# Seven half-size products a weight slot in eight late stages of a two-block transformer kernel, on a ring of three slots

## The reference

```
z = proj[..., g_end:].reshape(B_, L, N_BRANCH, N_KV, HPG, HEAD_DIM)
o = jnp.sum(gates * jax.nn.silu(z) * o_br, axis=2)
return o.reshape(B_, L, ATT_WIDTH) @ w_o
...
y_a = _gated_deltanet(q_a, k_a, v_a, z_a, beta_a, dec_a, conv_w[l], a_log[l], dt_bias[l], gdn_o_norm_w[l])
y_b = _moba_attention(q_b, k_b, v_b, q_norm_w[l], k_norm_w[l], rel_bias)
mix = (jax.nn.sigmoid(gate_a) * jnp.einsum('btc,cd->btd', y_a, w_branch_gdn[l])
       + jax.nn.sigmoid(gate_b) * jnp.einsum('btc,cd->btd', y_b, w_branch_moba[l]))
h = h + jnp.einsum('btd,de->bte', mix, w_out[l])
u = _rmsnorm(h, norm_ffn_w[l])
hid = jax.nn.silu(jnp.einsum('btd,df->btf', u, w_ffn_gate[l])) * jnp.einsum('btd,df->btf', u, w_ffn_up[l])
h = h + jnp.einsum('btf,fd->btd', hid, w_ffn_down[l])
```

## Time and profile before

| | |
|---|---|
| median of three runs | 3459.02 us |
| profiled execution, its own time | 3459.03 us |
| span of its core in the trace | 3457.1 us |
| TensorE busy | 3270.6 us, 95% of the span |
| VectorE, ScalarE, GpSimd busy | 1424.6, 474.7, 127.6 us |
| read from HBM | 593.7 MB, 173 GB/s over the span |
| `zc` stage | 1035 to 1148 us |
| attention with `zs` | 1148 to 1485 us |
| `o` and its norm | 1488 to 1620 us |
| `gdn`, `za`, `qb`, `kb`, `vb` | 1620 to 2046 us |
| scan with `ga` | 2046 to 2227 us |
| head norms and `gb` | 2227 to 2300 us |
| moba with `gb2` | 2300 to 2374 us |
| `bra`, `brb`, mix | 2374 to 2494 us |
| `out2` and its norm | 2494 to 2621 us |
| feed-forward part | 2621 to 3457 us |

### The profile page before, as it was taken

The page is one execution under the profiler, slowest core; times in us unless marked ns, Lnnn a source line. Parts: engine busy times, 40 slices in busy tenths (PEclk is TensorE's granted clock), DMA queues, the critical chain, the costliest instruction groups (busy, mean ns, idle before and its releaser), DMA issues.

```text
span 3457.1 us, 50025 instructions
## 1 busy us (share of the span) xinstructions
PE 3270.6 (95%) x20868; PEld 2894.0 (84%) x20868; DVE 1424.6 (41%) x2155; ACT 474.7 (14%) x799; POOL 127.6 (4%) x89
## 2 busy tenths in 40 slices
PE   6999998979999999988999999999898999999999
PEld 4777787868888877777888887688787999999999
DVE  5456625453220233313266731251104555555443
ACT  2114410000000222211220011311000000000000
POOL 0013310000000000011000000000000000000000
PEclk8999999989999999998999999999999999999999
DMA  9764377656563322232235332233432444444443
GB/s 409 296 262 162 157 281 300 249 220 249 228 275 125 139 101 97 97 122 109 111 144 182 149 138 94 98 130 108 172 146 103 168 167 170 170 170 164 172 163 133
DMA packets 50908, 598.73 MB, mean 173 GB/s; under 512 B 9511, under 2 KB 12086, under 8 KB 13278
## 3 DMA queue, kind: packets, MB, share of 16 engines
q1 hardware_dynamic: 50782, 596.88, 44.7%
HBM read 593.70 MB, written 3.16 MB: 173 GB/s over the span
## 4 chain that ended last, share of the span: by engine, by line
PE 84%; DMA 8%; DVE 5%; ACT 1%; DVEq 1%; issue 1%; SPq 0%; ACTq 0%; POOLq 0%; POOL 0%
PE bank L271 29%; PE bank L2037 23%; PE bank L301 13%; DMA ring<-in_t_mod 6%; PE bank L292 5%; PE bank L313 3%; DVE E L341 3%; PE bank L379 1%; PE bank L2051 1%; PE aux L1226 1%; PE aux L1181 1%; DMA ring<-in_t_out 0%; DMA ring<-in_t_kv 0%; DMA ring<-in_t_q 0%; PE aux L861 0%
## 5 line engine op out<-in xcount | busy, mean ns | idle before, releaser
L271 PE MATMUL bank<-arena,ring 128*128 128x256 f32 x3072 | 681.6, 385 | 43.2 <-DVE arena L1955 10.0
L271 PEld LDWEIGHTS bank<-arena,ring 128*128 128x128 f32 x3072 | 592.3, 193 | 129.7 <-issue 29.9
L271 PE MATMUL bank<-hT,ring 128*128 128x256 f32 x2560 | 561.5, 382 | 8.5 <-DVE hT L625 4.6
L271 PEld LDWEIGHTS bank<-hT,ring 128*128 128x128 f32 x2560 | 489.6, 192 | 77.6 <-issue 5.6
L301 PE MATMUL bank<-hT,ring 128*128 128x256 f32 x2304 | 533.0, 384 | 0.0
L301 PEld LDWEIGHTS bank<-hT,ring 128*128 128x128 f32 x2304 | 430.2, 191 | 75.2 <-issue 20.6
L2037 PE MATMUL bank<-arena,ring 128*128 128x128 f32 x3440 | 396.4, 275 | 0.0
L2037 PEld LDWEIGHTS bank<-arena,ring 128*128 128x128 f32 x3440 | 390.2, 192 | 0.0
L2037 PE MATMUL bank<-hT,ring 128*128 128x128 f32 x1680 | 197.9, 275 | 0.0
L2037 PEld LDWEIGHTS bank<-hT,ring 128*128 128x128 f32 x1680 | 192.7, 192 | 0.1
L341 DVE SCALAR_TENSOR_TENSOR E<-ring,c_act,E 128x512 f32<-128x512 f32 x240 | 182.8, 762 | 18.5 <-issue 0.6
(11 more groups left out here) (385 smaller groups left out, 2873.3 us busy)
## 6 DMA issues: line engine op xcount, KB each, us to landing
ring<-in_t_mod SPq DMA_DIRECT2D x64, 2048.0 KB, 13.9
ring<-in_t_gu SPq DMA_DIRECT2D x44, 2048.0 KB, 8.5
ring<-in_t_out SPq DMA_DIRECT2D x16, 2048.0 KB, 8.6
ring<-in_t_zs SPq DMA_DIRECT2D x16, 2048.0 KB, 8.5
ring<-in_t_down SPq DMA_DIRECT2D x16, 2048.0 KB, 7.3
ring<-in_t_gdn SPq DMA_DIRECT2D x12, 2048.0 KB, 8.4
ring<-in_t_u SPq DMA_DIRECT2D x8, 2048.0 KB, 9.9
ring<-in_t_z SPq DMA_DIRECT2D x8, 2048.0 KB, 8.5
```

The source lines that it names most:

```text
L271: last = nc.tensor.matmul(bank[s][:, T * f:T * f + T], w[:, j, P * f:P * f + P], act[:, j, :], start=j == 0, stop=j == kd - 1)
```

## The change

Eight stages (`zc`, `o`, `ga`, `gb`, `gb2`, `bra`, `brb`, `out2`) take their slots as the feed-forward part does: seven products of half the size (`late_split`), in all 37 full slots and 12 half-size ones (`SPLIT`; slot 0 of `o`, `ga`, `bra`, `out2` and slots 0, 4, 7 of `brb` stay plain). From `zc` to the end the ring has three places (`late_raw`), the fourth holds two of the weight sums for two slots (`late_spare`); the other two are written over the slot itself. A place is reloaded as soon as PE is done with it (`late_done`), no longer after the drain, and a slot now has a pair of banks, so that PE waits for the drain of the slot two before (`wait_out`). Two of the four weight sums are made by GpSimd (`pool_sums`) in all of these stages but `o` and `out2`, where VectorE makes them. The attention's and the scan's loops over groups and heads are written out. The sigmoid or SiLU of a split slot is a ScalarE pass over SBUF after VectorE has put the slot together (`late_act`).

The head norms go by rows: the sums of 12 blocks are put in four groups of 32 partitions of three banks (`pe_norm_sums`, 12 matmuls with 32 columns of weights), one root of 128x1536 and two reciprocals (128x512, 128x1024) follow, and three times four matmuls with one row of weights (`pe_norm_wide`) spread them again. `pe_norm_sums` and `pe_bias` stand after `gb`'s slot 0. The mix goes by slot: each slot of `bra` and `brb` is multiplied by its gate, and in `brb` added, as soon as it is done.

```diff
+LATE = [("zc", 8), ("zs", 16), ("o", 8), ("gdn", 12), ("za", 4), ("qb", 4), ("kb", 4), ("vb", 4),
+        ("ga", 8), ("gb", 4), ("gb2", 4), ("bra", 8), ("brb", 8), ("out2", 8)]
+LRING = 3
+LBASE = {n: sum(c for _, c in LATE[:k]) for k, (n, _) in enumerate(LATE)}
+LCOUNT = dict(LATE)
+LSLOTS = sum(c for _, c in LATE)
+EARLY = sum(n for _, n in ORDER)
+SPLIT = {"zc": range(8), "o": range(1, 8), "ga": range(1, 8), "gb": range(4), "gb2": range(4),
+         "bra": range(1, 8), "brb": (1, 2, 3, 5, 6), "out2": range(1, 8)}
+SPLITS = [(n, k) for n, _ in LATE if n in SPLIT for k in SPLIT[n]]
+SPLIT_INDEX = {x: m for m, x in enumerate(SPLITS)}
+ACTED = ("zc", "ga", "gb", "gb2")
+ACT_BASE = {n: sum(len(SPLIT[m]) for m in ACTED[:k]) for k, n in enumerate(ACTED)}
...
+        def late_ready(pe, n):
+            pe.wait_ge(late_in[n % LRING], 16 * (n // LRING + 1))
+            if n < 2:
+                for s in (2 * n, 2 * n + 1):
+                    wait_early(pe, s)
+            else:
+                wait_out(pe, n - 2)
...
+        def late_load(sp, name, k, count=SLOT):
+            n = LBASE[name] + k
+            if n < LRING:
+                wait_early(sp, (EARLY + n) % RING)
+            else:
+                sp.wait_ge(late_done, n - LRING + 1)
+            sp.dma_start(late_raw[n % LRING][:, 0:count], t["t_" + name][k]).then_inc(late_in[n % LRING], 16)
...
+            t1, t2, t3, t4 = t_all
+            one, two = late_bank(n)
+            if first == 0:
+                late_ready(pe, n)
+            end = 7 * half if count is None else first + count
+            for step in range(first, end):
+                q, j = step // half, step % half
+                if step == 0:
+                    pe.wait_ge(halves_ready, halves[0])
+                if q == 2 and j == 0:
+                    pe.wait_ge(late_sums, m + 1)
+                if q == 4 and j == 0:
+                    pe.wait_ge(halves_ready, halves[1])
+                if q == 5 and j == 0:
+                    pe.wait_ge(late_last, m + 1)
+                out, at, a, b = ((one, 0, w[:, 0, 0], x[0][0]), (one, 1, w[:, 1, 0], x[1][0]), (one, 2, s2, t2),
+                                 (two, 0, s1, t1), (two, 1, w[:, 0, 1], t3), (two, 2, w[:, 1, 0], x[1][1]),
+                                 (two, 3, w[:, 1, 1], t4))[q]
+                last = nc.tensor.matmul(out[:, P * at:P * at + P], a[:, j, :], tile_at(b, j),
+                                        start=j == 0 and q in (0, 3), stop=j == half - 1 and q in (2, 6))
+                if j == half - 1 and q == 1:
+                    last.then_inc(late_second, 1)
+                if j == half - 1 and q == 2:
+                    last.then_inc(late_first, 1)
+                if step == 7 * half - 1:
+                    last.then_inc(late_done, 1)
...
+        def late_keep(act, name, k):
+            n, m = LBASE[name] + k, SPLIT_INDEX[name, k]
+            loop_wait(act, late_first, m + 1)
+            nc.scalar.copy(join_keep[n % 2], late_bank(n)[0][:, 0:P]).then_inc(late_kept, 1)
...
+        def dve_sums(dve, name, k, parts=(0, 1)):
+            v, m = nc.vector, SPLIT_INDEX[name, k]
+            n = LBASE[name] + k
+            w, (s1, s2) = late_weights(name, k), late_two_sums(name, k)
+            if (name, k) in POOLED:
+                if 1 in parts:
+                    dve.wait_ge(late_pooled, POOLED.index((name, k)) + 1)
+            elif 0 in parts:
+                if m == 0:
+                    wait_early(dve, (EARLY + LRING) % RING)
+                dve.wait_ge(late_in[n % LRING], 16 * (n // LRING + 1))
+                if m > 1:
+                    old, at = SPLITS[m - 2]
+                    dve.wait_ge(late_done, LBASE[old] + at + 1)
+                v.tensor_tensor(s1, w[:, 0, 1], w[:, 1, 1], ALU.add)
+                dve.drain()
+                v.tensor_tensor(w[:, 0, 1], w[:, 0, 0], w[:, 0, 1], ALU.subtract)
+            if 1 in parts:
+                v.tensor_tensor(s2, s1, w[:, 0, 0], ALU.subtract)
+                dve.drain().then_inc(late_sums, 1)
...
+        POOLED = [(n, s) for n in ("zc", "ga", "gb", "gb2", "bra", "brb") for s in SPLIT[n]]
+        def pool_sums(pool, names):
+            for name, s in POOLED:
+                if name not in names:
+                    continue
+                n, m = LBASE[name] + s, SPLIT_INDEX[name, s]
+                w, (s1, s2) = late_weights(name, s), late_two_sums(name, s)
+                if m == 0:
+                    wait_early(pool, (EARLY + LRING) % RING)
+                pool.wait_ge(late_in[n % LRING], 16 * (n // LRING + 1))
+                if m > 1:
+                    old, at = SPLITS[m - 2]
+                    pool.wait_ge(late_done, LBASE[old] + at + 1)
+                nc.gpsimd.tensor_tensor(s1, w[:, 0, 1], w[:, 1, 1], ALU.add)
+                pool.drain()
+                nc.gpsimd.tensor_tensor(w[:, 0, 1], w[:, 0, 0], w[:, 0, 1], ALU.subtract)
+                pool.drain().then_inc(late_pooled, 1)
...
+        def dve_last_sum(dve, name, k):
+            m, w = SPLIT_INDEX[name, k], late_weights(name, k)
+            dve.wait_ge(late_second, m + 1)
+            nc.vector.tensor_tensor(w[:, 1, 0], w[:, 1, 0], late_two_sums(name, k)[1], ALU.subtract)
+            dve.drain().then_inc(late_last, 1)
+        def dve_join(dve, name, k, to):
+            v, n, m = nc.vector, LBASE[name] + k, SPLIT_INDEX[name, k]
+            one, two = late_bank(n)
+            dst = to.rearrange("p f n -> p (f n)")
+            dve.wait_ge(late_kept, m + 1)
+            v.tensor_tensor(dst[:, 0:P], one[:, P:2 * P], join_keep[n % 2], ALU.add)
+            v.tensor_tensor(join_two, one[:, 2 * P:3 * P], join_keep[n % 2], ALU.add)
+            dve.drain()
+            dve.wait_ge(late_done, n + 1)
+            v.tensor_tensor(join_pair.rearrange("p (a n) -> p a n", a=2), two[:, 0:2 * P].rearrange("p (a n) -> p a n", a=2),
+                            rep(join_two, 2), ALU.add)
+            dve.drain()
+            v.tensor_tensor(dst[:, P:3 * P], two[:, 2 * P:4 * P], join_pair, ALU.add)
+            v.tensor_tensor(dst[:, 3 * P:4 * P], two[:, 0:P], join_pair[:, P:2 * P], ALU.add)
+            dve.drain().then_inc(late_out[n % 2], 1)
...
         def pe_scan(pe):
...
+                def fill(plain, split):
+                    nonlocal done
+                    if h:
+                        late_split(pe, "ga", h, h_quarters, h_halves, (H_H, H_H3), done, split)
+                    else:
+                        late_plain(pe, "ga", h, hT, done, plain)
+                    done += split if h else plain
+                fill(7, 12)
...
+        def dve_norms(dve):
             v = nc.vector
+            v.tensor_scalar(q_scaled, col("q_norm"), SCALE, None, ALU.mult)
+            dve_last_sum(dve, "gb", 0)
+            dve_sums(dve, "gb", 1)
+            dve.wait_ge(norm_roots, 1)
+            v.reciprocal(norm_rows[:, 0:512], norm_rows[:, 0:512])
+            dve.drain().then_inc(norm_inv, 1)
+            v.reciprocal(norm_rows[:, 512:1536], norm_rows[:, 512:1536])
+            dve.drain().then_inc(norm_inv, 1)
+            for s in range(2):
+                dve_join(dve, "gb", s, two_tiles(gb_all, s))
+                dve_last_sum(dve, "gb", s + 1)
+                dve_sums(dve, "gb", s + 2)
+                dve.wait_ge(norm_wide, s + 1)
...
+        def dve_mix(dve):
...
+                if s in SPLIT[name]:
+                    dve_join(dve, name, s, two_tiles(to, s))
+                    v.tensor_tensor(two_tiles(to, s), two_tiles(to, s), two_tiles(gate, s), ALU.mult)
...
+                if name == "brb":
+                    v.tensor_tensor(two_tiles(x, s), two_tiles(x, s), two_tiles(y, s), ALU.add)
+            dve.drain().then_inc(mix_ready, 1)
...
             for n in range(FRING):
-                wait_old(sp, (FIRST_FFN + n) % RING)
+                sp.wait_ge(late_done, LSLOTS - LRING + n + 1)
                 load(n, gu[n])
```

559 lines of the change are left out of this document (399 added, 160 removed).

## The result

The changed kernel takes 3397.22 us (median of four runs, 3396.16 to 3398.61); the kernel before, with one more run, 3457.24. The ratio is 0.9829, 95% interval 0.9812 to 0.9846: 60.0 us less, where 56.4 were forecast (from 3459.02, the median that the forecast had). The profiled execution has a span of 3395.3 us, against 3457.1.

What follows compares the result with a forecast made beforehand. TensorE, 84% of the chain, was taken to bound the kernel. Terms of -56.3, +1.5, -11.1, +0.3, +0.3, +1.8, +5.6 and +1.5 summed to -56.4 from 3459.02: 3402.6 us, range 3384 to 3432.

Steps and rivals of the forecast that it cites:

- Products, -56.3: In the split stages, 37 full slots save 1.31 us each and 12 half-size ones 0.655: -56.3 us.
- Mix, -11.1: Ahead of `out2`, mixing by slot leaves about 2.0 us of 10.03 idle and 3.05 of slow start: -11.1 us.
- Feed-forward start, +5.6: After `out2`, slot 2's later load and four sums delay VectorE's reciprocal, and TensorE waits: +5.6 us (0 to +9).
- Norms, +0.3: Around `gb`, a 6.3 us wait for `rel_in`, bias, spreads, slow start and queries: 17.8 against 17.5, +0.3 us (-6 to +14).
- Equations, +1.2 of the scan's +0.3: At the scan's start, equations 12.8 us later make TensorE idle 2.7 at `ga`: first transpose +1.2; whole scan +0.3 us.
- Moba, +1.8: In moba, 0.9 us for VectorE held up by GpSimd and 0.9 for the bank wait ahead of `bra`: +1.8 (0 to +8).
- GpSimd beside VectorE, +1.5 in `brb`: In `brb`'s five slots, VectorE loses time to GpSimd on the shared port, 0.3 us a slot: +1.5 (bounds nothing to 6.6).
- I cost it at nothing: GpSimd's two sums a slot, outside `o` and `out2`, fit in the slack and cost nothing; without cover, 140 us.
- Rival 2: Norm matmuls run in turn (+14), or a tenth to a quarter of GpSimd's 140 us shows: 3412 to 3438 us; 20%.
- Rival 3: TensorE waits for GpSimd's sums before the third product in six stages: slower, all 140 us giving 3543; 5%.
- Half sums ahead of `zc`, +0.4: At `zc`'s start, a join or a pass is added behind the last product: +0.4 us.
- Attention, +0.5: At the attention's start, a join or a pass is added behind the last product: +0.5 us.

Runs made afterwards that it cites:

- e7: The kernel before, with only the attention's loop over four groups written out on three engines: 3440.20 us, ratio 0.9955.
- all repairs: The changed kernel with equations, tables and root first and GpSimd held back: 3370.58 us; with the norms' reciprocals in three parts as well: 3364.25 us.

## Why the prediction was right, and where it wasn't

The time, its sign and the range hold: 3397.2 against 3402.6 (3384 to 3432). The terms:

- **Products, -56.3: right.** 12.51 and 6.25 us a slot in each stage, also where GpSimd makes two sums; undone in 14 slots they cost 18.3. Only `zc`'s slot 0 gains less (15.1 us against 15.8), since PE's clock is still low there.
- **Mix, -11.1: right.** -8.4 for the gap and -2.8 for `out2`'s start.
- **Feed-forward start, +5.6: right.** +5.2; undone, -6.5.
- **Norms, +0.3: 3 too low, the mechanism right.** The wait for the tables is 5.7 (6.3). Missing were 1.9 of the wait ahead of moba (GpSimd beside VectorE: held back, 2.1 go), 0.9 of the bias product (1.87, at a low clock) and 0.6 of the spreads (1.07 each); the slow start was 2.2 (a slot of 14.7), put at 3.0. That the reciprocals lie bare once the tables are early was worked out at 5 and measured at 4.8.
- **Equations, +1.2 of the scan's +0.3: too low.** The 12.8 us are 14.4, the idle time 4.9 instead of 2.7, and the slow start behind it (1.8) was not in the sum; nor were the wait of 2.0 and the low clock of 1.6 behind it. Head 0 lost 7.3 us in all; the other seven won 2.4 beyond their products, where I had put 2.5 for PE's waits for ScalarE, which are gone.
- **Moba, +1.8: +2.7.** The wait ahead of `bra` is 0.8 (0.9); 1.6 are its first products at a low clock behind the wait for VectorE, which the sum did not have; what the sum had, 0.9 for VectorE held up, is then at most 0.3.
- **GpSimd beside VectorE, +1.5 in `brb`: the wrong place and size.** In `brb` it is 0.1. The runs tie some 11 us to it elsewhere: waits of 8.6, ahead of `zc`, in head 0 and ahead of moba, and 2.8 at a low clock behind the first two. The step that failed is "I cost it at nothing" and its slack, which asked only whether the sums come in time. They do: PE never waits for them. But where VectorE has a row of sums of its own on PE's path and GpSimd has two slots to catch up on, each VectorE sum waits for one of GpSimd's: 3.2 us instead of 1.2. Rows 6 gave the price (up to one GpSimd instruction each time they meet); I counted the meetings in the stages and not at their starts. Rival 2, which also rested on rows 6, meant another thing, slots that grow because the sums come late, and that didn't happen. Rival 3's break-even is miscounted: 56.4 us over 35 slots are 1.6 us a slot; the 4 that the prediction gives are all 140.
- **Half sums ahead of `zc`, +0.4: wrong**, +3.4, for that reason. At 1.23 us each they are hidden under the gates.
- **Attention, +0.5: wrong**, -7.2. I had passed over "loops written out" for the attention. It moves ScalarE's table load ahead of a wait, and PE's four waits at the groups' ends get 6.4 us shorter. I had taken this for the scan alone, as "half of 5.2", without its cause.
- **End of `o`, +0.6: -0.2**, nothing.
- **`gdn` to `vb`, nothing: -4.2,** of which 2.8 are scatter between two profiles of before, in a stretch of low clock; and **ahead of the gates, -1.8,** scatter. No step spoke of them.

So the total is nearer than its parts, and that is luck. Over the rows of the table the profiles lie 12 us above the forecast in some stages (3.0 ahead of `zc`, 4.5 in the scan, 2.8 in the norms) and 17 below it in others (the attention 7.7, `gdn` to `vb` 4.2, ahead of the gates 1.8). What the products and the two seams at the mix and the feed-forward start gave is the prediction's own.

## What to carry to other kernels

When work goes to GpSimd, don't ask only whether it is done in time. Look for VectorE's sums of two SBUF operands on the critical path in the same microseconds, above all at a stage's start, where GpSimd catches up; three semaphore waits that hold GpSimd back there brought 17 us in the medians (some 11 of them by this), where leaving GpSimd out altogether brought 9. A wait of TensorE can cost more than its own length: of those 11, 2.8 are the low clock behind it. When a ring gets shorter or loads wait for another event, follow what stands behind those loads on the same queue: sending the equations ahead of one load took 8.6 us off the scan's first head. And a loop around ScalarE can hold a table load behind a wait. When a sum of many terms comes out right, look at the stages before you trust the terms.

## What the runs showed of the hardware

- A VectorE sum of 128x1024 of two SBUF operands takes 1.23 us alone, and 3.2 beside a GpSimd sum of the same size, which then takes 3.1 instead of 2.36. They take turns: ahead of `zc` a pair comes every 3.3 us, so GpSimd's sums are not held up much, but VectorE makes one sum in a time in which it makes two and a half alone.
- ScalarE's table load takes 1.28 us, and where it stands to the wait depends on whether the wait is on a constant or a register's value. At the end of a group of the attention it begins behind 5.54 us of waiting in before; in e7 it is done 4.15 us before the product is there.
- After 4.9 us of idle time PE's next 5 us had a granted clock of 0.67, and its 14 records took 4.98 us instead of 3.2; after 5.7 us a slot took 2.2 longer; after 3.5 us, in another kernel, the clock was 1.00. After 2.0 us in head 0 it was 0.66 for 5 us, after 1.6 at the same place (equations first) 1.00; after 1.6 at the mix the slot took 0.3 longer. After 2.1 us ahead of moba it was 1.00 with GpSimd's waits alone and 0.66 with all repairs. So idle times of much the same length were followed by a low clock in one kernel and not in another, and these rows don't say why.
- Two programs with the same instructions up to the gates (e7 and before) differ there by 5 to 8 us in two profiles of each, for the most part at five waits. The cause stays open.
